# Two transformer layers on one core: modulation rows spread to one per weight slab, gates stored as sigmoids, gate halves loaded apart, attention steps moved a slab later

## The chip, the core and the metric

The kernel runs on one core of a Trainium2 chip, in fp32 from inputs to output. What counts is the device time of one execution, in microseconds (us). An engine's instructions run in its own order, and the engines wait for each other by semaphores: TensorE (PE) multiplies, VectorE (DVE) and ScalarE (ACT) do elementwise work, GpSimd (POOL) and SyncE (SP) issue most of the transfers from memory.

## The reference

256 tokens of width 2048 pass through two layers.

```python
# layer 1
mod = silu(c) @ w_ada + b_ada                 # 3 parts of 2048: shift, scale, gate
h = rmsnorm(x, pre_g) * (1 + scale) + shift
q, k, v, gate_a, u, gate_p = split(h @ w_in)
y_a = windowed_gqa(q, k, v) * silu(gate_a)    # 8 heads of 128
y_p = multiscale_pool(u) * silu(gate_p)
g_a, g_p = split(sigmoid(h @ w_merge + b_merge))
x = x + gate * rmsnorm((g_a * (y_a @ w_br_attn) + g_p * (y_p @ w_br_pool)) @ w_out)
# layer 2
mod = silu(c2) @ w_mod + b_mod                # 6 parts of 2048
...                                           # attention with 16 heads of 64, gated linear attention (GLA) with 4 heads
merged = sigmoid(g_a) * (o_a @ w_br_a) + sigmoid(g_b) * (o_b @ w_br_b)
x = x + g1 * rmsnorm(merged @ w_out)
h = rmsnorm(x) * (1 + sc2) + sh2
x = x + g2 * rmsnorm((silu(gate) * val) @ w_down)   # gate, val = conv(h @ w_up), width 5632
```

## The kernel before

**Weights in slabs.** All large products run as a row of 368 slabs, numbered through the program. A slab is 4 x 128 rows by 512 columns of weights, 1 MB. SP loads it to `w_stage` (5 buffers, `load_slab`, 3 slabs ahead). Since fp32 is multiplied as two halves of its bits, ACT rounds the slab to `w_hi` (`split_hi`, two instructions of 128x1024, 3 buffers), and DVE computes the rest to `w_lo` (`split_lo`, two instructions). Both do this `AHEAD` = 2 slabs before PE needs it, and `split_hi(n)` waits until PE has finished slab n-3. PE's `gemm(n)` runs 16 pairs of matmuls on a slab, (hi, 512 columns) and (lo, 256 columns), into the four PSUM tiles `gemm`. A group of 4 slabs (2 or 4 in the branches, 11 at the end) makes one result of 4 tiles. Then the group is evacuated in two pairs: ACT copies the low half out (`evac_low`), DVE adds the high half (`evac`), and the next group's first matmul on these tiles waits for that (`wait_evac`).

**Phases and hooks.** A `Phase` has one or two groups. All other work is tied to slabs of a phase: `hooks[s]` are run by every engine behind its part of slab s, `late` and `post` behind the phase, `pre` ahead of it. On each engine the order in a slab is: the split of slab s+2, the hooks of s, the modulation rows of s, and the evacuation if the group ends. Nothing else sets the order; each engine keeps to this list, and what waits holds up all behind it. The phases in order: u0, u1, in (4), in_gates (2), gate_p1, merge (8), branch1 (4), out1 (4), kv2, gk, q2 (2), qkvb (4), og (4), gates2 (4), branch2 (4), out2 (4), up (11), down (4). Ahead of u0, kv2 and up stands `prep_h`, which normalises and modulates h and makes its 16 operand tiles.

**Modulation rows.** `mod` is a vector times a matrix. Parts 0 and 1 are made before the first slab. Parts 2 to 8 are made beside the phases: a row is 128 x 2048 weights, loaded in two halves to `mod_stage` (one buffer for each half, `load_mod_row`: a half's load waits until DVE has used what stood there), and DVE adds it, times a column of c, to `mod_acc` (`mod_row`, two instructions of 128x1024). `mods_behind` spreads the rows of a phase evenly over the slabs that do not end a group; four rows on three such slabs put two behind the first. Behind a part's 16 rows PE sums over partitions (`mod_end`, 16 matmuls with one column each), and POOL clears `mod_acc`.

**Gates.** The merge gates of a layer are stored to memory before the sigmoid (`gate_out`, `store_gate`), as 8 groups of 4 tiles. In the phases branch1 and branch2 both halves (for the attention branch and for the other) are loaded together to `gate_in` when the phase before is merged, ACT takes the sigmoid of both (`gl_sig`), and `evac` multiplies with them, the first half behind slab 1.

**Attention.** A head (layer 1) or a pair of heads (layer 2) takes five steps: attn1 scores (PE); attn2 bias, row maximum (DVE) and exp (ACT); attn3 normalisation (DVE) and transposes (PE); attn4 copy (ACT) and product with v (PE); attn5 the operand (ACT, DVE). They stand behind slabs 0, 1, 2, 3 of a phase, and `late`. GLA has steps gla0 to gla7 in gates2; gla2 prepares on DVE and multiplies on PE behind the same slab.

Of the kernel before, what the change touches and what calls it, by code (L numbers as in the profile page):

```python
# [18 lines left out]
ALU = mybir.AluOpType  # L19
# [3 lines left out]
P = 128  # L23
# [70 lines left out]
class Phase:  # L94

    def __init__(self, name, i, groups, hooks=None, late=(), mod=None, pre=(), post=()):
        self.name, self.i, self.groups, self.hooks, self.late = name, i, groups, hooks or {}, late
        self.mod, self.pre, self.post = mod, pre, post
        self.slabs = [(g, q) for g in groups for q in range(g.slabs)]


def build(nc, A, out):
    ctx = ExitStack()
    with ctx:
# [119 lines left out]
        phases.append(Phase("gate_p1", 0, [one(4096)], mod=(3, 0, 3), post=[("silu1", 0), ("v1", 0)]))  # L224
        for i in range(8):
            arg = dict(blk=1, kv=i // 4, u=i)
            phases.append(Phase("merge", i, [Group(w_merge, 512 * i, 4, "main", "gate", bias=col["b_merge"] + 4 * i, slot=4 * i)],
                                hooks=attn(0, arg), late=[("attn5", arg)], mod=(3, 3 + 2 * i, 2) if i < 5 else (3, 8 + i, 1),
                                post=[("mod_end", 3)] if i == 7 else []))
        for i in range(4):  # L230
            phases.append(Phase("branch1", i, [Group(A["w_branch_attn"][0], 512 * i, 2, "attn", "merge_a", n=i),
                                               Group(A["w_branch_pool"][0], 512 * i, 2, "main", "merge_b", n=i)],
                                hooks={0: [("gl_sig", i)], **({2: [("merged_hi", (0, 0)), ("merged_hi", (0, 1))]} if i == 3 else {})},
                                mod=(4, i, 1), pre=[] if i else [("poolmix", 0), ("prep_y", 1)]))
# [1463 lines left out]
```

## Time and profile before

| | |
|---|---|
| median of 3 runs | 2533.04 us (2531.62 to 2541.36) |
| the profiled execution | 2532.78 us, span of its instructions 2531.0 us |
| mean granted clock of PE | 0.949 |
| busy: PE / DVE / ACT / POOL | 2313.1 / 1745.9 / 1103.2 / 93.8 us |
| moved | 580.55 MB, mean 229 GB/s |

Busy time is the time in which an instruction of the engine runs. The granted clock is the share of PE's full clock (2.4 GHz) that the chip lets through: 1.0, or 0.5 (1.2 GHz) after PE has stood still or done little; a mean over a stretch lies between. The profile gives times from the first instruction on. "Idle before, releaser" is the time an engine stood still before an instruction, and what ended it.

### The profile page before, as it was taken

What the parts mean: (1) busy time and instruction counts of PE and PEld (TensorE: products, weight loads), DVE (VectorE), ACT (ScalarE), POOL (GpSimd) and SP (SyncE); (2) the same over time, 40 slices, a digit from 0 to 9 for tenths busy, and PEclk for the clock granted to TensorE, in tenths of its full rate; (3) what the DMA queues carried; (4) which work ended last, traced back from release to release, by engine and by line L of the source; (5) the groups of instructions that cost most, each with busy time, mean ns of one, the idle gap of its engine ahead of it and who ended that gap; (6) DMA issues with size and microseconds to landing.
All of it is one profiled execution on the core that took longest, in us unless ns stands there. A gap on an engine that the chain in (4) does not pass through costs nothing. (4 is left out here: it accounts for less than half of the span.)

```text
span 2531.0 us, 31212 instructions
## 1 busy us (share of the span) xinstructions
PE 2313.1 (91%) x12880; PEld 1991.0 (79%) x12880; DVE 1745.9 (69%) x2015; ACT 1103.2 (44%) x1406; POOL 93.8 (4%) x112
## 2 busy tenths in 40 slices
PE   2499999999898899998999979988999999999998
PEld 1378788887777777787888868877888888888887
DVE  5877766767777677667766676776777777774443
ACT  1243344444445554443344443344444444444443
POOL 1000000010000000000011100000000000000000
PEclk7599999999999999998999989998999999999999
DMA  9967778776684756668866676784555555565553
GB/s 359 387 209 276 263 238 277 267 249 239 241 307 133 252 178 206 217 223 297 306 230 225 234 250 222 268 312 146 183 183 184 188 190 187 183 217 183 182 177 108
DMA packets 245089, 580.55 MB, mean 229 GB/s; under 512 B 11850, under 2 KB 14718, under 8 KB 240596
## 3 DMA queue, kind: packets, MB, share of 16 engines
q1 hardware_dynamic: 232320, 535.86, 61.3%
q0 software_dynamic: 11296, 40.20, 4.5%
q10 hardware_dynamic: 1332, 2.51, 0.3%
q8 instruction: 101, 1.65, 0.3%
q14 instruction: 40, 0.33, 0.0%
HBM read 557.55 MB, written 20.97 MB: 229 GB/s over the span
## 5 line engine op out<-in xcount | busy, mean ns | idle before, releaser
L1646 PE MATMUL gemm<-operand_main,w_hi 128*128 128x512 f32 x4311 | 1576.7, 406 | 82.1 <-DVE merge_part L1328 30.3
L1647 PE MATMUL gemm<-operand_main,w_lo 128*128 128x256 f32 x4311 | 1222.8, 284 | 0.0
L1015 DVE TENSOR_TENSOR w_lo<-w_stage,w_hi 128x1024 fp32r<-128x1024 f32 x736 | 860.9, 1212 | 468.9 <-ACT w_hi L670 468.2
L670 ACT ACTIVATE w_hi<-w_stage 128x1024 fp32r<-128x1024 f32 x736 | 732.6, 1045 | 783.7 <-PE gemm L1647 683.2
L1646 PEld LDWEIGHTS gemm<-operand_main,w_hi 128*128 128x128 f32 x4311 | 827.6, 192 | 279.6 <-DVE w_lo L1015 72.6
L1647 PEld LDWEIGHTS gemm<-operand_main,w_lo 128*128 128x128 f32 x4311 | 831.2, 193 | 13.6
L1009 DVE SCALAR_TENSOR_TENSOR mod_acc<-mod_stage,c_silu,mod_acc 128x1024 f32<-128x1024 f32 x224 | 280.9, 1281 | 83.1 <-DMA mod_stage<-in_w_mod 49.3
L1646 PE MATMUL gemm<-ffn_hidden,w_hi 128*128 128x512 f32 x688 | 242.9, 397 | 0.0
L1646 PE MATMUL gemm<-operand_attn,w_hi 128*128 128x512 f32 x480 | 181.2, 416 | 15.5 <-DVE proj L1316 15.5
L1647 PE MATMUL gemm<-ffn_hidden,w_lo 128*128 128x256 f32 x688 | 192.5, 280 | 0.0
L1646 PEld LDWEIGHTS gemm<-ffn_hidden,w_hi 128*128 128x128 f32 x688 | 129.1, 188 | 29.4
L1647 PE MATMUL gemm<-operand_attn,w_lo 128*128 128x256 f32 x480 | 139.0, 290 | 0.0
L1647 PEld LDWEIGHTS gemm<-ffn_hidden,w_lo 128*128 128x128 f32 x688 | 129.8, 189 | 0.8
L1646 PEld LDWEIGHTS gemm<-operand_attn,w_hi 128*128 128x128 f32 x480 | 95.5, 199 | 38.7 <-DVE w_lo L1015 16.7
L1650 PE MATMUL gemm<-operand_main,w_hi 128*128 128x512 f32 x313 | 125.5, 401 | 0.0
L1647 PEld LDWEIGHTS gemm<-operand_attn,w_lo 128*128 128x128 f32 x480 | 95.8, 200 | 1.6
L670 ACT ACTIVATE proj<-gemm 128x512 f32<-128x512 f32 (+1 forms) x73 | 43.3, 595 | 110.0 <-PE gemm L1650 109.9
L1649 PE MATMUL gemm<-operand_main,w_lo 128*128 128x256 f32 x313 | 88.7, 283 | 0.0
L1316 DVE TENSOR_TENSOR proj<-gemm,proj 128x512 f32<-128x512 f32 (+1 forms) x57 | 38.5, 685 | 54.0 <-ACT proj L670 54.0
L1649 PEld LDWEIGHTS gemm<-operand_main,w_lo 128*128 128x128 f32 x313 | 59.2, 189 | 15.4
L1322 DVE TENSOR_TENSOR gate_out<-gemm,gate_out 128x512 f32<-128x512 f32 x40 | 27.4, 691 | 54.4 <-ACT gate_out L670 54.3
L1650 PEld LDWEIGHTS gemm<-operand_main,w_hi 128*128 128x128 f32 x313 | 59.8, 191 | 0.0
(211 smaller groups left out, 1475.0 us busy)
## 6 DMA issues: line engine op xcount, KB each, us to landing
w_stage<-in_w_in SPq DMA_DIRECT2D x128, 1024.0 KB, 6.2
mod_stage<-in_w_mod SPq DMA_DIRECT2D x192, 512.0 KB, 6.0
w_stage<-in_w_up SPq DMA_DIRECT2D x88, 1024.0 KB, 5.0
w_stage<-in_w_down SPq DMA_DIRECT2D x44, 1024.0 KB, 5.0
w_stage<-in_w_ada SPq DMA_DIRECT2D x32, 1024.0 KB, 11.2
w_stage<-in_w_merge SPq DMA_DIRECT2D x32, 1024.0 KB, 6.0
w_stage<-in_w_out SPq DMA_DIRECT2D x32, 1024.0 KB, 7.8
mod_stage<-in_w_ada SPq DMA_DIRECT2D x32, 512.0 KB, 5.9
```

The source lines that it names most:

```text
L670: return nc.scalar.activation(o, i_, f, **kw)
L1009: stt(acc, MST[:, half, :], CSI[:, c:c + 1], acc, ALU.mult, ALU.add).then_inc(mod_rows, 1)
L1015: tt(WL[:, slot_of(n), c0:c1], WST[:, slot_of(n), c0:c1], WH[:, n % HIS, c0:c1].bitcast(F32), ALU.subtract)\
L1316: tt(o, high, o, ALU.add).then_inc(pair_done, 1)
L1322: tt(o, high, o, ALU.add).then_inc(pair_done, 1)
L1646: mm(G[:, m, :], hi, x_of(k), start=(k == 0), stop=False)
L1647: ins = mm(G[:, m, T:2 * T], lo, x_of(k)[:, 0:T], start=False, stop=False)
L1649: mm(G[:, m, T:2 * T], lo, x_of(k)[:, 0:T], start=False, stop=False)
L1650: ins = mm(G[:, m, :], hi, x_of(k), start=False, stop=True)
```

## The change

1. `slots` says behind which slabs the rows stand, at most one row per slab; the parts are dealt anew over the phases (og1 to og3 and out2 have 3 rows and no longer 4; gates2 has its rows late in a phase; mod_end of part 6 moves one phase on).
2. A part's first row is written by `tensor_scalar` and not added, so POOL's clearing of `mod_acc` is gone.
3. ACT takes the sigmoid of a gate group in `gate_out` before it is stored (`gate_sig`, behind slab 0 of the next phase, and behind slab 4 in gates2), 16 instructions of 128x1024. `store_gate` waits for it. `gl_sig` is gone.
4. The two halves of `gate_in` are loaded apart (`load_gates`), the attention half of phase i+1 as soon as that of phase i is multiplied.
5. PE's transposes (`attn_turn`) stand one slab later than DVE's attn3; attn4 and attn5 move behind slabs 0 and 1 of the next phase (slabs 4 and 5 within qkvb), the last head's stay `late`. The product with v goes to another PSUM tile, so that the next scores wait for less. PE's half of gla2 (`gla_pairs`) stands one slab later; gla7 moves from slab 1 to 2, the last head's gla6 and gla7 into branch2.
6. `poolmix`, `prep_y1` and `prep_y2` become hooks. 
7. In `prep_h` the splits of slabs 0 to 2 (0 to 3 in all) stand before or within the loop over operand tiles and not behind it.

```diff
-        attn = lambda o, a: {o + s: [(f"attn{s + 1}", a)] for s in range(4)}
+        attn = lambda o, a: {o: [("attn1", a)], o + 1: [("attn2", a)], o + 2: [("attn3", a)], o + 3: [("attn_turn", a)]}
+        def with_tail(hooks, at, a):
+            return {**hooks, at: [("attn4", a)] + hooks.get(at, []), at + 1: [("attn5", a)] + hooks.get(at + 1, [])}
...
-            phases.append(Phase("in_gates", i, [one(2048 + 1536 * i)], mod=((2, 11, 4), (2, 15, 1))[i],
+            phases.append(Phase("in_gates", i, [one(2048 + 1536 * i)], mod=((2, 11, 3), (2, 14, 2))[i],
...
-                                mod=(6, 4 * i - 4, 4) if i else (5, 14, 2), post=[] if i else [("mod_end", 5)]))
+                                hooks={} if i else with_tail({}, 0, head2[7]),
+                                mod=(6, 3 * i - 3, 3) if i else (5, 15, 1), post=[] if i else [("mod_end", 5)]))
...
-                                late=[("gla6", 3), ("gla7", 3)] if i == 3 else [], mod=((6, 12, 4), (7, 0, 3), (7, 3, 3), (7, 6, 3))[i], post=[] if i else [("mod_end", 6)]))
+                                       2: [("gla2", i)] + ([("gla7", i - 1)] if i else []), 3: [("gla_pairs", i)],
+                                       4: [("gate_sig", 8 + 2 * i), ("gla3", i)], 5: [("gla4", i)], 6: [("gla5", i)]},
+                                mod=((6, 9, 3), (6, 12, 4), (7, 0, 3), (7, 3, 3))[i], slots=(4, 5, 6, 2),
...
-            free = [n for n, (g, q) in enumerate(ph.slabs) if q < g.slabs - 1]
-            return [r for r in range(rows) if free[r * len(free) // rows] == s]
+            slots = ph.slots or [n for n, (g, q) in enumerate(ph.slabs) if q < g.slabs - 1]
+            return [r for r in range(rows) if sorted(slots[:rows])[r] == s]
...
+            def load_gates(blk, half, i):
+                n = i + 4 * blk
+                pool.wait_ge(gate_stored, 16 * ((0, 12)[blk] + 4 * half + i + 1))
+                if half:
+                    positive(pool, merge_tiles, 2 * n)
+                else:
+                    positive(pool, part_merged, n)
...
-                if name == "gl_sig":
-                    act.wait_ge(gates_in, 32 * arg + 32)
-                    activate(GL[:, :, :, :], GL[:, :, :, :], ACT.Sigmoid).then_inc(sig_ready, 1)
+                if name == "gate_sig":
+                    g = sig_groups[arg]
+                    o = GST[0 if arg < 8 else 1]
+                    wait_evac(act, g)
+                    activate(o[:, :, :], o[:, :, :], ACT.Sigmoid).then_inc(gate_sig, 1)
...
+                    for ahead in range(2 if k else 0, 3):
+                        split_lo(ph.slab0 + ahead)
...
+                        if s == 11:
+                            split_lo(ph.slab0 + 3)
```

DVE at the start of u0, before the change: the loop over operand tiles (`quad_work`, `operand_main`), then the splits (`w_lo`), 12 instructions on end. Rows are the instructions in the engine's order, with their lines.

```order
L1042 SCALAR_TENSOR_TENSOR affine_cols<-mod_cols,columns 128x16
L1058 SCALAR_TENSOR_TENSOR quad_work<-proj,affine_cols,rstd 128x256 x3
L1062 SCALAR_TENSOR_TENSOR operand_main<-quad_work,mod_cols,operand_main 128x256
...
L1062 SCALAR_TENSOR_TENSOR operand_main<-quad_work,mod_cols,operand_main 128x256 x3
L1015 TENSOR_TENSOR w_lo<-w_stage,w_hi 128x1024 x12
```

And with the change:

```order
L1086 SCALAR_TENSOR_TENSOR affine_cols<-mod_cols,columns 128x16
L1059 TENSOR_TENSOR w_lo<-w_stage,w_hi 128x1024 x6
L1106 SCALAR_TENSOR_TENSOR quad_work<-proj,affine_cols,rstd 128x256 x3
L1110 SCALAR_TENSOR_TENSOR operand_main<-quad_work,mod_cols,operand_main 128x256
...
L1059 TENSOR_TENSOR w_lo<-w_stage,w_hi 128x1024 x2
...
L1110 SCALAR_TENSOR_TENSOR operand_main<-quad_work,mod_cols,operand_main 128x256 x3
L1059 TENSOR_TENSOR w_lo<-w_stage,w_hi 128x1024 x4
```

Six halves (slabs 0 to 2) moved ahead of the loop, two (slab 3) into it.

DVE in the phase og2, before: the splits, the modulation rows (`mod_acc`, two instructions each) and the evacuation to `gate_out`.

```order
L1015 TENSOR_TENSOR w_lo<-w_stage,w_hi 128x1024 x2
L1009 SCALAR_TENSOR_TENSOR mod_acc<-mod_stage,c_silu,mod_acc 128x1024 x4
L1015 TENSOR_TENSOR w_lo<-w_stage,w_hi 128x1024 x2
L1009 SCALAR_TENSOR_TENSOR mod_acc<-mod_stage,c_silu,mod_acc 128x1024 x2
L1015 TENSOR_TENSOR w_lo<-w_stage,w_hi 128x1024 x2
L1009 SCALAR_TENSOR_TENSOR mod_acc<-mod_stage,c_silu,mod_acc 128x1024 x2
L1015 TENSOR_TENSOR w_lo<-w_stage,w_hi 128x1024 x2
L1322 TENSOR_TENSOR gate_out_87<-gemm,gate_out_87 128x512 x2
```

And with the change:

```order
L1059 TENSOR_TENSOR w_lo<-w_stage,w_hi 128x1024 x2
L1053 SCALAR_TENSOR_TENSOR mod_acc<-mod_stage,c_silu,mod_acc 128x1024 x2
L1059 TENSOR_TENSOR w_lo<-w_stage,w_hi 128x1024 x2
L1053 SCALAR_TENSOR_TENSOR mod_acc<-mod_stage,c_silu,mod_acc 128x1024 x2
L1059 TENSOR_TENSOR w_lo<-w_stage,w_hi 128x1024 x2
L1053 SCALAR_TENSOR_TENSOR mod_acc<-mod_stage,c_silu,mod_acc 128x1024 x2
L1059 TENSOR_TENSOR w_lo<-w_stage,w_hi 128x1024 x2
L1371 TENSOR_TENSOR gate_out_87<-gemm,gate_out_87 128x512 x2
```

The second row behind slab 0 is gone, the others stand where they stood.

ACT at slab 0 of gates2, phase 2, with the change: `gla_v` is gla6's sigmoid, the rows `gla_q` to `gla_k_end` gla0's exponentials. Before, the same rows stood there without the second one, and each ACT_TABLE_LOAD too.

```order
L701 ACTIVATE w_hi<-w_stage 128x1024 x2
L701 ACTIVATE gate_out_87<-gate_out_87 128x1024
L701 ACT_TABLE_LOAD
L701 ACTIVATE gla_rstd<-extra,small 128x256
L701 ACT_TABLE_LOAD
L701 ACTIVATE gla_v<-gla_out_gate 128x1024
L701 ACT_TABLE_LOAD
L701 ACTIVATE gla_q<-gla_diff 128x512
L701 ACTIVATE gla_k<-gla_diff 128x512
...
L701 ACTIVATE w_hi<-w_stage 128x1024 x2
```

One instruction, the sigmoid of the gate group before, moved in ahead of the table loads.

## Rows read from the trace of the kernel before

**Rows 1.** The page: busy time (parts 1 and 5).
```profile
PE 2313.1 (91%) x12880; PEld 1991.0 (79%) x12880; DVE 1745.9 (69%) x2015; ACT 1103.2 (44%) x1406; POOL 93.8 (4%) x112
L1009 DVE SCALAR_TENSOR_TENSOR mod_acc<-mod_stage,c_silu,mod_acc 128x1024 f32<-128x1024 f32 x224 | 280.9, 1281 | 83.1 <-DMA mod_stage<-in_w_mod 49.3
```

**Rows 2.** Windows at slab ends: us, busy (count), PEclk, DMA share, GB/s.
```profile
275.10:329.00 53.90, 47.75 (x259) 41.21 (x259) 33.48 (x30) 18.13 (x20) 0.00 (x0) 0.94 0.74 261
591.30:676.60 85.30, 74.04 (x386) 63.61 (x385) 57.76 (x63) 37.24 (x42) 4.49 (x6) 0.92 0.64 223
951.30:1115.40 164.10, 156.94 (x915) 129.82 (x915) 114.14 (x152) 77.43 (x138) 0.00 (x0) 1.00 0.61 212
1151.60:1234.10 82.50, 72.17 (x386) 62.34 (x385) 62.28 (x59) 29.57 (x34) 2.27 (x3) 0.94 0.93 328
1279.30:1291.70 12.40, 12.40 (x65) 11.30 (x66) 8.58 (x11) 9.89 (x12) 4.94 (x3) 0.72 0.41 139
1303.60:1311.00 7.40, 7.40 (x62) 6.59 (x62) 5.52 (x7) 2.61 (x3) 0.00 (x0) 1.00 0.47 154
1336.80:1452.40 115.60, 105.19 (x626) 91.87 (x625) 83.30 (x102) 54.84 (x64) 12.56 (x10) 0.96 0.66 227
1354.50:1368.70 14.20, 9.05 (x61) 8.00 (x62) 11.11 (x20) 2.61 (x3) 0.80 (x1) 0.88 0.39 137
1452.40:1579.20 126.80, 107.99 (x580) 93.08 (x578) 87.03 (x88) 55.44 (x60) 8.09 (x8) 0.91 0.68 233
1619.40:1733.50 114.10, 101.22 (x536) 86.77 (x534) 78.23 (x72) 47.60 (x59) 1.16 (x1) 0.94 0.80 281
1852.50:1897.80 45.30, 45.30 (x258) 39.29 (x257) 34.66 (x48) 20.41 (x22) 0.00 (x0) 1.00 0.57 186
```

**Rows 3.** Waits of PE: us in total, times, longest us.
```profile
PE gemm L1646 <- DVE merge_part L1328: 30.3, 7, 10.8
PE gemm L1646 <- DVE proj L1316: 28.3, 6, 6.6
PE gemm L1646 <- DVE w_lo L1015: 19.2, 4, 16.0
PE extra L1565 <- DVE scores L1237: 18.0, 11, 4.4
PE gemm L1646 <- DVE gate_out L1322: 10.3, 3, 3.7
PE extra L1601 <- DVE gla_k_end L1280: 7.6, 2, 3.8
```

**Rows 4.** Timeline of DVE at the start of u0.
```profile
115.97 1.28 DVE L1058 SCALAR_TENSOR_TENSOR quad_work<-proj,affine_cols,rstd 128x256 f32<-128x256 f32 x3
129.06 2.36 DVE L1015 TENSOR_TENSOR w_lo<-w_stage,w_hi 128x1024 fp32r<-128x1024 f32 x2 [0.34 <-ACT w_hi L670]
```

**Rows 5.** Timeline of DVE in og2.
```profile
1179.62 1.28 DVE L1009 SCALAR_TENSOR_TENSOR mod_acc<-mod_stage,c_silu,mod_acc 128x1024 f32<-128x1024 f32 x1 [2.72 <-DMA mod_stage<-in_w_mod]
```

**Rows 6.** DMA issues in 1145 to 1235: KB each, us to landing.
```profile
w_stage<-in_w_in SPq DMA_DIRECT2D x14, 1024.0 KB, 7.9
mod_stage<-in_w_mod SPq DMA_DIRECT2D x26, 512.0 KB, 5.3
```

**Rows 7.** Timeline of DVE in gates2, phase 3 (starts at 1394.6).
```profile
1407.11 2.36 DVE L1015 TENSOR_TENSOR w_lo<-w_stage,w_hi 128x1024 fp32r<-128x1024 f32 x2 [0.72 <-ACT w_hi L670]
1420.35 2.36 DVE L1015 TENSOR_TENSOR w_lo<-w_stage,w_hi 128x1024 fp32r<-128x1024 f32 x2
```

**Rows 8.** Timeline of ACT at its slab 0.
```profile
1397.09 1.28 ACT L670 ACT_TABLE_LOAD   x1
1398.39 0.48 ACT L670 ACTIVATE gla_rstd<-extra,small 128x256 f32<-128x256 f32 x1
```

**Rows 9.** Timeline of DVE in qkvb0.
```profile
921.69 0.69 DVE L1316 TENSOR_TENSOR proj<-gemm,proj 128x512 f32<-128x512 f32 x1 [0.97 <-ACT proj L670]
```

**Rows 10.** Lines of ACT by form: busy us, mean ns; idle before.
```profile
L670 ACT ACTIVATE gla_v<-gla_out_gate 128x1024 f32<-128x1024 f32 x4 | 4.2, 1061 | 0.0
```

More of the change, by code:

```diff
@@ L223, in build @@
                                 post=[("mod_end", 2)] if i else []))
-        phases.append(Phase("gate_p1", 0, [one(4096)], mod=(3, 0, 3), post=[("silu1", 0), ("v1", 0)]))
+        phases.append(Phase("gate_p1", 0, [one(4096)], mod=(3, 0, 2), slots=(1, 2), post=[("silu1", 0), ("v1", 0)]))
+        head1 = [dict(blk=1, kv=u // 4, u=u) for u in range(8)]
         for i in range(8):
-            arg = dict(blk=1, kv=i // 4, u=i)
+            behind = attn(0, head1[i])
+            if i:
+                behind = with_tail(behind, 0, head1[i - 1])
+                behind[0] = behind[0] + [("gate_sig", i - 1)]
+            if i == 6:
+                behind[2] = behind[2] + [("poolmix", 0)]
@@ L234, in build @@
-                                mod=(4, i, 1), pre=[] if i else [("poolmix", 0), ("prep_y", 1)]))
+                                hooks=behind, mod=(4, i, 1)))
         for i in range(4):
@@ L307, in build @@
                 merged_from.append(ph.slab0 + 2)
+        by_tile_phases = [ph for ph in phases if ph.name in ("u0", "kv2", "up") and ph.i == 0]
         named = lambda name: [ph for ph in phases if ph.name == name]
@@ L387, in build @@
         MA = proj_tile("merge_part", [P, QUAD, T], F32, 52)
-        gate_stored, gates_in, sig_ready = sem("gate_stored"), sem("gates_in"), sem("sig_ready")
+        gate_stored, gate_sig, part_merged = sem("gate_stored"), sem("gate_sig"), sem("part_merged")
+        gates_in = [sem("gates_a_in"), sem("gates_b_in")]
         merge_tiles = sem("merge_tiles")
+        sig_groups = [g for ph in phases if ph.name in ("merge", "gates2") for g in ph.groups]
         WP = proj_tile("w_pool", [P, 4, 2, 2 * P], F32, 40)
@@ L781, in stage @@
                     norm_root(n)
+                    if k == 0:
+                        for first_slab in range(3):
+                            split_hi(first_slab)
                     shift = (0, 3, 6)[k] * KT
@@ L957, in _ @@
                 for s, (g, q) in enumerate(ph.slabs):
-                    if ph.slab0 + s + AHEAD < len(slabs):
+                    if ph.slab0 + s + AHEAD < len(slabs) and not (ph in by_tile_phases and s < 2):
                         split_hi(ph.slab0 + s + AHEAD)
@@ L1627, in gemm @@
                     pe.wait_ge(op_ready, op_count[name] - g.slabs + q + 1)
-                if g.operand == "attn" and q == 0:
-                    pe.wait_ge(y_done, 8 if ph.name == "branch1" else 16)
+                if g.operand == "attn" and ph.i == 0:
+                    pe.wait_ge(y_done, 4 * q + 4 + (0 if ph.name == "branch1" else 8))
                 if g.operand == "hid":
```

151 lines of the change are left out of this document (86 added, 65 removed).

## The prediction

> **What bounds the kernel now.** I read the page first: PE is busy for 91% of the span, DVE for 69%, ACT for 44% [rows 1]. So PE is the bound, and the question is where it stands still. A window without a wait gives its pace: 8 slabs in 45.30 us at clock 1.00, 5.66 us a slab (5.65 below) [rows 2] (its last row). 368 slabs at that pace are 2079 us, so some 450 us are start, small matmuls, waits and half clock. The waits of PE name the waits [rows 3]: on the splits at the start (19.2, of which 16.0 once), on `merge_part` (30.3 in 7), `proj` (28.3 in 6), the attention's `scores` (18.0 in 11), `gate_out` (10.3 in 3) and GLA's `gla_k_end` (7.6 in 2).
>
> Then I cut the trace at slab ends. Last three phases of og: 82.50 us for 12 slabs, which are 67.8 at the pace [rows 2]. The loss is 14.7, the wait only 10.3 [rows 3]; the window's clock is 0.94. A wait of some 3.5 us thus costs about 1.5 more, because the granted clock then falls to its lower level (1.2 GHz) for a while: (14.7 − 10.3) / 3. Below, a wait of over 2 us counts with 1.5 to 1.7 more. The same subtraction prices each place.
>
> What is late there: DVE takes a half of a modulation row only when its transfer has landed (it waits 2.72 us for it) [rows 5], a half takes 5.3 us to land [rows 6], and there is one buffer for each half. All DVE has to do behind it, the evacuation last, waits too. What is removed is counted only where it frees this chain; DVE's 280.9 us on rows [rows 1] stay.
>
> **The change part by part.**
>
> *Start of u0.* The loop begins at 115.97 and the last splits at 129.06, which end at 131.4, when PE's wait ends [rows 4]. The six halves take 3 x 2.3 = 6.9 us and now stand ahead of the loop; ACT makes its halves while DVE and PE still work on `mod`, so I add nothing for it. The gemm may begin behind the first operand tile, about 1.6 us later: 115.97 + 6.9 + 1.6 = 124.5. Gain 131.4 − 124.5 = 6.9, say **7.0**. (The later operand tiles are made faster than PE takes a slab.)
>
> *Rows, at most one behind a slab.* Let a phase begin at T, the end of PE's slab before. ACT's and DVE's split put DVE's first row at about T + 3.4; the next row starts a landing plus 1.5 us later; so three rows, and the split behind them, end at T + 3.4 + 2 (L + 1.5) + 2.5 + 2.4 = T + 11.3 + 2L. With L = 5.3 [rows 6] that is T + 21.9, against four slabs' end T + 22.6; some semaphore steps add up to 1 us. It is about level, so I leave 1.0 a phase and no half clock. For og: 14.7 − 3 = 11.7, **12** with the few tenths that lie in front. in_gates: 53.90 − 8 x 5.65 = 8.7, leave 1: **7.5**. Out of layer 2: 114.10 − 16 x 5.65 − three `mod_end`-like sums of 1.7 = 18.6 [rows 2]; its first phase still has late rows behind a long evacuation, so I leave 6: **12.6**.
>
> *Gates.* In branch1 (12 slabs) 85.30 − 67.8 = 17.5 [rows 2], three waits on `merge_part` [rows 3]: ACT and DVE wait for both halves to land and ACT for its sigmoid. With the attention half loaded a phase early, and no sigmoid there, DVE has it ahead of time: **17.5**. Branch2 (18 slabs): 126.80 − 101.7 = 25.1 [rows 2], of which 10.8 idle is the first phase's [rows 3]. There ACT's chain stays long: two table loads of 1.28 and the new sigmoid of 1.06 [rows 8, 10] come before the operand and the split, and DVE follows 15.5 us behind the phase's start where PE needs it at 2 slabs, 11.3. 4.2 and 1.7 for the clock remain, about 6: **19.3**.
>
> The sigmoids cost 16 x 1.06 = 17 us of ACT [rows 10], which is idle 56% of the span [rows 1]; two table loads each more would be some 18 loads x 1.28 = 23 us. Both lie in slab 0, where ACT has more than 3 us to spare, but in gates2.
>
> *gates2.* The window of phases 2 and 3 is 115.60 us [rows 2]. A slab with GLA work and no wait is 7.40 [rows 2] (from 1303.60), slab 3 of phase 2 is 14.20, so 6.8 lost, twice: the two waits on `gla_k_end`, 3.8 each [rows 3], and 1.4 for `gla_k`. Moving PE's half a slab back removes both: +6.9 each. But the new sigmoid delays ACT's chain of three table loads by 1.06, and gla7 and a late row move to DVE's slab 2. For phase 3, from T = 1394.6: the splits that began at 1407.11 begin at T + 13.6; from there to the end of the splits of 1420.35 (1422.6) lie 15.5 us of DVE work [rows 7], of which one row of 2.4 moves away: T + 26.7, and 0.7 for the first evacuation. PE asks at 4 x 5.65 + 2.6 = T + 25.2. A new wait of about 2.2, with clock 3: net +3.9. Phase 1 has four rows, one in slab 2: wait 4.7 + 1.7 = −6.5, new. Phase 2 has `mod_end` (12.40 − 5.65 = 6.7, which leaves phase 1 [rows 2] (from 1279.30)) at its start, which gives DVE slack: +6.9. Sum **+4.3**. Without the cover of `mod_end` phase 2 would give 3 less.
>
> A rule of the Trainium skill speaks against this part. The row: a table load takes 1.28 us, from 1397.09, and the next ACT instruction starts at 1398.39, so 0.02 later [rows 8]. The page "ScalarE: Activation LUTs", section "What ACT_TABLE_LOAD costs", has 2.66 us for each switch, with a drain of 1.38. By the page the chain of loads would be some 4 us later at three places, and the result some 12 us higher, an estimate from that page. The trace disagrees with it here, and the sum goes by the row.
>
> *Attention.* The waits on `scores` are 18.0 in 11 [rows 3]: 5.1 in merge, 5.7 in qkvb0, and six of 1.2 later. Those of merge go with their clock, 5.1 + 1.6, less 1.1 of a new wait where the last head's product stands: **5.6**. qkvb1 to 3: 164.10 − 156.94 = 7.2 of idle at clock 1.00 [rows 2], all go. In qkvb0 DVE is late by itself: its evacuation starts at 921.69 [rows 9], where PE, freed of the wait, asks for it at 917.2; a wait of 4.1 takes its place. **6.9**.
>
> *prep_h of kv2 and up.* Splits in the loop remove the small waits behind its first slabs: **2.7**. A part's first row as `tensor_scalar` (half the time of a 1.28 us instruction at best, 14 of them) and POOL's clearing lie off the path: 0. poolmix and prep_y as hooks: 0, hidden behind slabs of PE; uncovered, some 2 us.
>
> Sum: 7.0 + 7.5 + 5.6 + 17.5 + 6.9 + 12 + 4.3 + 19.3 + 12.6 + 2.7 = 95.4. The profiled execution is 2532.78 us, 0.3 from the median of 2533.04. Time: 2532.8 − 95.4 = **2437 us**.
>
> Bounds of what the trace doesn't show: the left-overs of 1 us in rows (0 to 3.5 in 10 phases, −6 to +25), branch2's 6 (2 to 12), gates2's new waits (0 to 13 with clock, so −9 to +5), out's 6 (2 to 12). Together 2403 to 2470.
>
> **The rivals.**
> (A) *Clean:* all named gaps go and nothing takes their place: 12 + 6 + 9.5 + 4.1 + 3 of left-overs less, **2403**. For it: DVE has 31% free. Against it: the arithmetic in gates2 and branch20.
> (B) *The transfer stays the bound:* three rows in neighbouring slabs reload the same buffer, L is not 5.3 but 6 and more, and og, out2, in_gates and branch2 each keep 2 to 4 us a phase and the half clock. 7 to 10 phases of 3.5 more: **2465** (2455 to 2490). For it: slabs' loads land in 7.9 us in the same stretch [rows 6]. The page "Perfetto Trace Analysis" of the Trainium skill, section "Optimization Strategy", says that the same gap repeating can mean too few buffers. The change adds none.
> (C) *Slower:* the same mechanism, worse: with one row behind every slab L reaches what the slab loads take there, 7.9. Then three rows end at T + 27.1, 4.5 late, and with clock 6.2 in each of about 25 phases with three rows: 155 us, **2590**. It decides for slower from L = 7 (some 4.3 us a phase eats 108 us). Against it: L is 5.3 where the DMA share is already 0.93 [rows 2, 6], and halving the burst in slab 0 lowers it.
> (D) *It does nothing:* waits only change place, since DVE's work is the same: 2525 to 2540. Against it: branch1's wait is for a load that is simply earlier.
>
> **How the numbers follow.** Forecast 0.59 (2415 to 2455), A 0.15, B 0.19, C 0.04, D 0.03. All but C and D are faster by far over 0.5%, about what a measurement of this kernel can tell from none. The range takes the better part of A and half of B: 2400 to 2472. Faster 0.93, same 0.03, slower 0.04.
>
> **What would show it.** The first gemm's wait 9 in place of 16; no wait of over 1 us on `merge_part` in layer 1; in og and in_gates waits of at most 1 us; qkvb1 to 3 without idle time; a wait of 4.1 on `proj` in qkvb0; new waits on `gate_out` in gates2, phase 1 (4.7) and 3 (2.2); one of 4 on `merge_part` in branch20, and one of 4 at out21. mod_stage's landing at 5.3 to 6. I am wrong if this landing grows past 6.5, if DVE's splits come late where ACT loads tables, or if the clock falls in places where no wait is.

## The result, and the profile after

The changed kernel takes 2448.47 us in the median of 4 runs (2441.76 to 2450.23), the kernel before 2536.86 us beside it (2531.62 to 2541.36). The ratio is 0.9647, with a 95% interval of 0.9617 to 0.9678: faster, by 3.5% or some 88 us. I had forecast 2437 (2400 to 2472), 95 us less. The two profiled executions differ by 82.7 us of span (2531.0 and 2448.3); that of the changed kernel is the longest of its four (1.8 above their median), that of the kernel before lies 4.1 below its median, so the profiles show some 6 us less than the medians.

The page of the changed kernel, busy time by engine:

```profile
PE 2286.6 (93%) x12880; PEld 1973.2 (81%) x12880; DVE 1742.4 (71%) x2015; ACT 1125.4 (46%) x1432; POOL 81.2 (3%) x105
```

The waits of PE in the changed kernel, as [rows 3]:

```profile
PE gemm L1699 <- DVE proj L1365: 26.1, 7, 6.8
PE gemm L1699 <- DVE operand_main L1110: 17.8, 3, 9.5
PE gemm L1699 <- DVE gate_out L1371: 10.0, 4, 4.9
PE gemm L1699 <- DVE merge_part L1377: 5.3, 1, 5.3
PE gemm L1699 <- DVE proj L1377: 4.7, 3, 3.1
```

The waits on `scores` and `gla_k_end` are gone, that on `w_lo` of 16.0 is one of 9.5 on `operand_main`, and of seven on `merge_part` one is left; `proj L1377` is the evacuation of the other branch's half, at the ends of branch2's phases: three waits, 4.7 in all, that the kernel before didn't have. Those on `gate_out` are others than before: 4.9 and 2.5 of the 10.0 us are the new ones in gates2, and 2.1 is one behind merge's first phase that nothing had forecast:

```profile
371.45 0.47 PE L1699 MATMUL gemm<-operand_main,w_hi 128*128 128x512 f32 x1 [2.12 <-DVE gate_out L1371]
```

Windows of the changed kernel, cut at slab ends like [rows 2]. In order: in_gates, branch1, qkvb1 to 3, og1 to 3 with gates2's first slab, gates2 phase 1, gates2 phases 2 and 3, branch2's first three phases, out2; then two that gained nothing or little, q2's second phase and qkvb0.

```profile
268.80:314.50 45.70, 45.16 (x260) 39.22 (x258) 33.62 (x30) 18.25 (x20) 0.00 (x0) 1.00 0.83 288
575.30:643.00 67.70, 67.70 (x386) 58.85 (x385) 57.25 (x62) 32.51 (x39) 3.76 (x5) 1.00 0.81 279
919.10:1074.90 155.80, 154.20 (x914) 129.80 (x913) 114.84 (x153) 76.22 (x138) 0.00 (x0) 1.00 0.67 223
1111.80:1180.50 68.70, 68.08 (x386) 58.71 (x386) 53.05 (x51) 28.17 (x32) 2.27 (x3) 1.00 0.90 314
1225.60:1282.90 57.30, 52.40 (x316) 45.80 (x314) 44.66 (x53) 30.68 (x35) 6.28 (x5) 0.97 0.74 248
1282.90:1395.40 112.50, 109.99 (x656) 96.60 (x656) 83.85 (x103) 61.45 (x70) 13.60 (x11) 0.95 0.71 238
1395.40:1509.80 114.40, 105.32 (x579) 90.86 (x577) 92.73 (x91) 51.25 (x58) 7.70 (x8) 0.96 0.82 288
1548.80:1652.80 104.00, 98.20 (x536) 84.88 (x536) 77.71 (x74) 47.71 (x59) 1.16 (x1) 0.97 0.86 304
836.10:862.50 26.40, 24.35 (x129) 21.09 (x130) 20.81 (x20) 18.48 (x17) 0.00 (x0) 0.94 0.82 288
862.50:919.10 56.60, 52.16 (x291) 43.88 (x290) 41.50 (x56) 32.63 (x51) 0.00 (x0) 0.94 0.50 168
```

Read them against [rows 2]: the length less PE's busy time is idle time; what the length loses beyond that is half clock. Branch1 is 67.70 long, all busy, at clock 1.00: no wait is left. Out2 still has 5.8 idle and a clock of 0.97. Gates2 is counted over its phases 1 to 3, branch2 as forecast over its first three phases and then its last. Place by place, in us (forecast, then measured):

| place | forecast | measured |
|---|---|---|
| first product's wait | 7.0 | 6.5 |
| in_gates | 7.5 | 8.2 |
| merge, to the first product of branch1 | 5.6 | 2.1 |
| branch1 | 17.5 | 17.6 |
| qkvb | 6.9 | 10.7 |
| og to gates2's first slab | 12 | 13.8 |
| gates2 | 4.3 | 3.3 |
| branch2, first three phases | 19.3 | 12.4 |
| branch2, last phase | 0 | 1.2 |
| out2 | 12.6 | 10.1 |
| kv2, up | 2.7 | 2.6 |
| q2, second phase | 0 | −3.8 |
| the rest, by subtraction | 0 | −2.0 |
| sum | 95.4 | 82.7 |

### The profile page after: what moved, and what is told of

Its sections match the earlier page's. It is cut to its first block, busy times and chain, and to the rows that moved or that the text cites. A ratio compares the mean times of both kernels' runs of the same rounds, so it can differ in the third digit from the quotient of the medians.

```text
span 2448.3 us, 31291 instructions
## 1 busy us (share of the span) xinstructions
PE 2286.6 (93%) x12880; PEld 1973.2 (81%) x12880; DVE 1742.4 (71%) x2015; ACT 1125.4 (46%) x1432; POOL 81.2 (3%) x105
## 4 chain that ended last, share of the span: by engine, by line
PE 78%; DVE 11%; DMA 7%; ACT 2%; issue 1%; ACTq 0%; DVEq 0%; SPq 0%
PE gemm L1699 46%; PE gemm L1700 23%; DVE w_lo L1059 3%; PE gemm L1703 3%; DMA mod_stage<-in_w_mod 3%; DMA w_stage<-in_w_ada 3%; DVE mod_acc L1053 2%; PE gemm L1702 1%; PE extra L1499 1%; DMA w_stage<-in_w_in 1%; PE extra L1492 1%; ACT w_hi L701 1%; PE extra L1631 1%; DVE mod_acc L1038 1%; PE extra L1607 1%
## 5 line engine op out<-in xcount | busy, mean ns | idle before, releaser
L1699 PE MATMUL gemm<-operand_main,w_hi 128*128 128x512 f32 x4311 | 1560.6, 403 | 49.7 <-DVE operand_main L1110 17.8
L1700 PEld LDWEIGHTS gemm<-operand_main,w_lo 128*128 128x128 f32 x4311 | 824.4, 191 | 13.5
L1053 DVE SCALAR_TENSOR_TENSOR mod_acc<-mod_stage,c_silu,mod_acc 128x1024 f32<-128x1024 f32 x210 | 267.1, 1301 | 49.3 <-DMA mod_stage<-in_w_mod 43.1
L1699 PE MATMUL gemm<-operand_attn,w_hi 128*128 128x512 f32 x480 | 180.4, 415 | 15.3 <-DVE proj L1365 10.7
L1699 PEld LDWEIGHTS gemm<-operand_attn,w_hi 128*128 128x128 f32 x480 | 95.0, 198 | 38.6 <-DVE w_lo L1059 16.8
L1703 PE MATMUL gemm<-operand_main,w_hi 128*128 128x512 f32 x313 | 124.6, 398 | 0.0
L1700 PEld LDWEIGHTS gemm<-operand_attn,w_lo 128*128 128x128 f32 x480 | 95.4, 199 | 1.5
L1365 DVE TENSOR_TENSOR proj<-gemm,proj 128x512 f32<-128x512 f32 (+1 forms) x57 | 38.6, 684 | 48.4 <-ACT proj L701 48.4
```

The lines of the kernel that those rows point to most:

```text
L1053: stt(acc, MST[:, half, :], CSI[:, c:c + 1], acc, ALU.mult, ALU.add).then_inc(mod_rows, 1)
L1365: tt(o, high, o, ALU.add).then_inc(pair_done, 1)
L1699: mm(G[:, m, :], hi, x_of(k), start=(k == 0), stop=False)
L1700: ins = mm(G[:, m, T:2 * T], lo, x_of(k)[:, 0:T], start=False, stop=False)
L1703: ins = mm(G[:, m, :], hi, x_of(k), start=False, stop=True)
```

## The experiments

Each kernel was timed beside the kernel before; the numbers are medians, the ratio to the kernel before, and its 95% interval. Changes of single places are read from windows or waits, since those of the whole are only known to some 5 us.

**The rows dealt as before (e1_rows_old).**

```diff
-            slots = ph.slots or [n for n, (g, q) in enumerate(ph.slabs) if q < g.slabs - 1]
-            return [r for r in range(rows) if sorted(slots[:rows])[r] == s]
+            free = [n for n, (g, q) in enumerate(ph.slabs) if q < g.slabs - 1]
+            return [r for r in range(rows) if free[r * len(free) // rows] == s]
...
-                                mod=(6, 3 * i - 3, 3) if i else (5, 15, 1), post=[] if i else [("mod_end", 5)]))
+                                mod=(6, 4 * i - 4, 4) if i else (5, 14, 2), post=[] if i else [("mod_end", 5)]))
```

and so in every phase.

> The changed kernel with the rows dealt over phases and slabs as before (four rows in og1 to og3 and out2, the first two behind one slab; mod_end of part 6 behind gates2 phase 1's predecessor). Theory, that the rows' transfers set these phases: in_gates +7, og +14, out2 +10, branch2 up to +5 come back, while q2 gives 3.8 and gates2 phase 1 and 3 give their new waits (6.5 and 4) back: about +22, 2470 us. Rival, that the gates' and the attention's edits did most of it, since they take work from the same engines at the same places: under +8, 2456 us or less.

2480.20 us, ratio 0.9773 (0.9748 to 0.9797): 32 us slower than the changed kernel. Its windows of in_gates, og and out2:

```profile
269.10:324.60 55.50, 47.04 (x259) 40.73 (x259) 33.85 (x31) 18.25 (x20) 0.00 (x0) 0.94 0.71 252
1116.20:1198.50 82.30, 72.02 (x387) 61.85 (x386) 61.73 (x59) 29.47 (x34) 2.27 (x3) 0.94 0.92 326
1568.80:1684.30 115.50, 100.17 (x537) 85.86 (x535) 78.19 (x72) 47.72 (x60) 1.16 (x1) 0.94 0.79 278
```

They are as long as before the change ([rows 2]: 53.90, 82.50, 114.10), whatever else was changed. The deal of the rows alone is worth about 32 of the 88 us, more than the 22 I expected, since gates2 got 6 us slower and not faster. Two places got faster: q2's second phase went from 26.4 back to 22.6, and branch2's first three phases from 114.4 to 111.8.

**Is it the transfer or DVE's amount of work? (e5_old_two_buffers).** The kernel before, with a second pair of buffers for 12 rows.

```diff
+        MST2 = at("mod_stage_b", [P, 2, D // 2], F32, o_ex)
...
-                    sp.dma_start(MST[:, half, :], w.rearrange("(c q) n -> c q n", q=P)[row0 + r, :, c0:c0 + D // 2])\
-                        .then_inc(m_landed[half], 16)
+                    sp.dma_start(buf[:, half, :], w.rearrange("(c q) n -> c q n", q=P)[row0 + r, :, c0:c0 + D // 2])\
+                        .then_inc(landed_, 16)
```

> The kernel before, with its four rows in each of og1 to og3, but these 12 rows go alternately to mod_stage and to a second pair of buffers in memory that the attention left free. Theory, that the reload of a single buffer is what makes DVE late: the three waits on gate_out (3.6, 3.0, 3.7) and their half clock go, -13 to -15 in og and gates2's start, 2519 us. Rival, that four rows are too much work for DVE in four slabs: the waits stay at 3 and more, 2533 us.

2527.69 us, ratio 0.9956 (0.9938 to 0.9974), 11 us less: under the 13 to 15 expected, but clear of noise. The window of og and the landings in it (KB each, median us to landing):

```profile
1156.50:1224.60 68.10, 68.06 (x386) 58.87 (x386) 58.07 (x56) 27.86 (x31) 2.27 (x3) 1.00 0.97 363
```
```profile
mod_stage_b<-in_w_mod SPq DMA_DIRECT2D x10, 512.0 KB, 9.2
mod_stage<-in_w_mod SPq DMA_DIRECT2D x10, 512.0 KB, 6.6
```

With the four rows a phase of before, 82.50 became 68.10 without a wait. So DVE's amount of work was never too much (it is busy for 58.07 of the 68.10); the reload of a single buffer was what came late. A single landing takes longer here than the 5.3 of [rows 6], with more transfers under way at once, and it does not matter. Gates2's last two phases and out2 are 2 us longer each in this profile, which is the rest between 14 and 11; why isn't shown. The rival of the prediction that pointed to the buffers had the mechanism right; the deal cures it in another way, by asking for fewer rows.

**The load of the gates put off (e2_gates_late), the sigmoid put back (e7_sigmoid_in_branch), and both (e8_both_back).**

```diff
-                if half:
-                    positive(pool, merge_tiles, 2 * n)
-                else:
-                    positive(pool, part_merged, n)
+                positive(pool, merge_tiles, 2 * n)
```
```diff
+                if name == "gl_sig":
+                    half, n = arg
+                    act.wait_ge(gates_in[half], 16 * n + 16)
+                    activate(GL[:, half, :, :], GL[:, half, :, :], ACT.Sigmoid).then_inc(gl_ready[half], 1)
...
-                        dve.wait_ge(gates_in[int(b)], 16 * n + 16)
+                        dve.wait_ge(gl_ready[int(b)], n + 1)
```

> The changed kernel with one wait put back: the attention half of the gates is loaded no earlier than the other half, when the phase before is merged; the sigmoid stays ahead of the store. Theory, that the early load is what frees branch1: waits on merge_part of about 2 us come back (3.8 before, less the sigmoid of 1.9 that no longer follows the load) in three phases of branch1 and two of branch2, with some clock: +10 to +14, about 2460 us. Rival, that the sigmoid's leaving the chain was enough: the load of 4.7 us ends before slab 1's end, nothing comes back, 2449 us.

2445.22 us, ratio 0.9639 (0.9614 to 0.9665), 3 us less than the changed kernel. No wait came back in branch1: my theory was wrong, its rival right. In branch2 a wait went away, that of 3.1 at the second phase, though the rows stand as in the changed kernel; see branch2 in the next section.

> The changed kernel with the sigmoid taken on the loaded gates again, half by half, behind slabs 0 and 2 (3 in layer 2), while the early load stays; gates are stored as before the sigmoid. Theory of the sum: branch1 stays without waits, and in gates2 the chain of ACT is 1.06 shorter, so that the waits of 4.9 and 2.5 there become 3.9 and 1.5, and branch20's 5.3 becomes 4.2: -3 to -7, about 2444 us. Rival, that taking the sigmoid off the branches was needed: waits on merge_part of 1 to 2 us come back in branch1 and branch2, +5 or more, 2454 us.

2446.96 us, ratio 0.9634 (0.9617 to 0.9651), 1.5 us less than the changed kernel and less of a gain than expected. No wait in branch1 here either. The waits of PE that gates2 and branch20 have:

```profile
PE gemm L1704 <- DVE gate_out L1376: 8.4, 4, 4.0
PE gemm L1704 <- DVE merge_part L1382: 4.3, 1, 4.3
```

The longest wait on `gate_out` went from 4.9 to 4.0, that on `merge_part` from 5.3 to 4.3: the sigmoid's 1.06 us on ACT passes into PE's waits almost whole, as the prediction's arithmetic had it.

> The two edits of the runs before together: attention half loaded only when the phase before is merged, and its sigmoid taken in the branch phase, behind slab 0; the halves are still two loads and two sigmoids. Neither edit alone brought a wait back. Theory, that load, sigmoid and product are one chain and each edit alone is enough to shorten it: now waits on merge_part of 2 to 4 us return in three phases of branch1, and in branch2, +10 to +17, about 2460 us. Rival, that it was the joint load and the joint sigmoid of 1.9 behind slab 0, with the split of the next slab queued behind it: split in halves the chain stays short, no waits over 0.5 in branch1, 2447 us.

2455.68 us, ratio 0.9676 (0.9654 to 0.9697), some 7 us above the changed kernel and 9 to 10 above the runs with one of the two edits. Waits of PE:

```profile
PE gemm L1704 <- DVE merge_part L1382: 14.8, 6, 4.4
```

In branch1 three waits of 1.5 to 1.7 are back, of 3.6 to 3.8 before. Neither theory holds alone. The early load and the early sigmoid stand in for each other and together are worth 1.6 a phase; the other 2.1 are not in these two edits. What then still differs from the kernel before is that the halves are loaded and turned into sigmoids apart (1.06 us of ACT each, not 1.92 behind a joint load) and the deal of the rows. That it is the former I only argue: branch1 has one row a phase in both kernels.

**PE's transposes with DVE's step again (e3_turn_early).**

```diff
-        attn = lambda o, a: {o: [("attn1", a)], o + 1: [("attn2", a)], o + 2: [("attn3", a)], o + 3: [("attn_turn", a)]}
+        attn = lambda o, a: {o: [("attn1", a)], o + 1: [("attn2", a)], o + 2: [("attn3", a), ("attn_turn", a)], o + 3: []}
```

> The changed kernel with PE's transposes behind the same slab as DVE's attn3 again; the later attn4 and attn5 and the other PSUM tile stay. Theory, that PE waited there for DVE: the waits on scores come back, 1.2 in each of 16 steps of qkvb's and 0.6 or less in merge's: +8 to +10, about 2458 us, with one of 4 in qkvb0 in the place of today's on proj. Rival, that the waits went because the next scores wait for less: no wait on scores, 2449 us.

2456.22 us, ratio 0.9672 (0.9642 to 0.9702), about 7 above the changed kernel, somewhat under the theory's range of 8 to 10. Waits of PE:

```profile
PE extra L1618 <- DVE scores L1286: 13.5, 9, 4.6
```

The waits on `scores` come back (18.0 in 11 before, [rows 3]), 4.6 of them in qkvb0 where the changed kernel has its wait on `proj`. The six later ones are 0.5 to 0.7 each, not 1.2; so about half of those was the looser order of the later steps. Both reasons hold. The 13.5 us cost only some 7, since waits of DVE's evacuations on `proj` and `gate_out` shrink by 8.9 beside them.

**The splits behind the loop (e4_splits_behind).**

```diff
-                    for ahead in range(2 if k else 0, 3):
-                        split_lo(ph.slab0 + ahead)
...
-                        if s == 11:
-                            split_lo(ph.slab0 + 3)
```

> The changed kernel with the splits of the first slabs behind the loop over operand tiles again, in u0, kv2 and up. Theory, the sum's terms of 7.0 and 2.7: the first product's wait grows from 9.5 to 16 and small waits in slabs 2 to 4 of kv2 and up come back: +8 to +10, about 2458 us. Rival, that the start is bound by the operand tiles, and PE would wait for them in slab 0 instead: +3 or less.

2451.65 us, ratio 0.9663 (0.9627 to 0.9700): in the total hardly to be told from the changed kernel. Waits of PE:

```profile
PE gemm L1692 <- DVE w_lo L1054: 17.6, 3, 16.0
```

The wait of 16.0 is back in place of 9.5, so the term of 7.0 is 6.5; kv2 is 1.2 longer and up 0.5.

**What was left: rows moved (e6_rows_moved), rows lightened (e9_rows_lightened), the decay moved (e10_decay_moved).** The first takes q2's third row and phase 1's fourth row in gates2 away; the second also takes one row each from the first phases of branch2 and out2.

```diff
-                                mod=((6, 9, 3), (6, 12, 4), (7, 0, 3), (7, 3, 3))[i], slots=(4, 5, 6, 2),
+                                mod=((6, 9, 4), (6, 13, 3), (7, 0, 3), (7, 3, 3))[i], slots=(4, 5, 6, 2),
```
```diff
-                                mod=((7, 6, 3), (7, 9, 3), (7, 12, 4), (8, 0, 4))[i], slots=(4, 2, 3, 0) if i else (2, 3, 4),
+                                mod=((7, 6, 2), (7, 8, 4), (7, 12, 4), (8, 0, 5))[i], slots=(4, 2, 3, 0, 1) if i else (2, 3),
```
```diff
-                behind[1] = behind[1] + [("gk_ln", 0)]
-                behind[2] = behind[2] + [("gk_cum", 0)]
-                behind[4] = behind[4] + [("swap", 2)]
+                behind[0] = behind[0] + [("gk_ln", 0)]
+                behind[4] = behind[4] + [("swap", 2), ("gk_cum", 0)]
```

> The changed kernel with q2 at two rows a phase (as before) and four in gates2 phase 0 in place of phase 1. Theory, that a row too many makes these two waits: the wait at the start of q2's second phase (2.0 and 1.7 of clock) and the one of 4.9 in gates2 phase 1 shrink, the latter to about 2.4 or less; phase 0 has no gla7 before it and takes its row without a wait: -6 to -9, about 2441 us. Rival, that the fourth row only moves the wait: phase 0 shows 3 to 5 us instead, 2445 to 2449 us.

2442.32 us, ratio 0.9621 (0.9602 to 0.9639). This is 6 less than the changed kernel, as the theory had it. The wait at q2's second phase is gone and that of 4.9 in gates2 is 2.5. Gates2's phase 0 took its fourth row without a wait: from its second slab to its end it's busy throughout, as in the changed kernel. A wait of 0.9 in front of it belongs to og3's evacuation; in two kernels whose phase 0 has three rows (e8_both_back, e12_pool_clears) one of 1.1 and 1.0 stands there too.

```profile
PE gemm L1699 <- DVE gate_out L1371: 8.1, 4, 2.5
```

> The run with the moved rows (q2, gates2), and further: two rows in branch2's first phase (for three), four in its second, five in its last, two in out2's first. Theory, that the third row, behind a late start of DVE, makes the waits of 3.0 at branch2's second phase and of 4.9 at out2's: both fall under 1 us, -3.0 - 1.7 - 4.9 - 2.5 less 1 of new waits: -11 against the run with moved rows, about 2431 us. Rival, that these phases are late by the operands' preparation, whatever the rows: out2's wait stays over 3, -5 or less, 2437 us or more.

2436.79 us, ratio 0.9597 (0.9577 to 0.9616), 5.5 less than the run before it, not 11. Against the changed kernel, out2's second phase went from 32.1 to 25.3 and branch2's second from 38.6 to 33.9, as expected; the four rows in branch2's second phase then made a wait of 1.8 at the third, with half clock, 2.8 in all, and one of 1.1 at the fourth, 1.3. From branch2's first product to out2's it's 154.4 us, 1.5 less than in the run before; most of the gain is out2's.

> The changed kernel with the decay's logarithm (ACT) at slab 0 of the first qkvb phase instead of slab 1, and its two DVE instructions of 3.5 us at slab 4 instead of 2. Theory, that they put off the evacuation at slab 3: the wait on proj of 4.4 us there and its 3.4 at half clock go: -5 to -6, about 2443 us, with at most 1 us of wait left. Rival, that the wait moves to the evacuation at slab 7, since DVE gets the scans there too: -1 to +1, 2448 us.

2447.50 us, ratio 0.9642 (0.9621 to 0.9664). The window of qkvb0:

```profile
862.40:911.90 49.50, 49.50 (x290) 41.93 (x290) 40.29 (x54) 32.89 (x50) 0.00 (x0) 1.00 0.57 190
```

It lost 7.1 us and all its idle time, and the phase behind it gained 2.9 (its first wait grew from 1.6 to 3.0, with half clock). Half of each theory: the wait goes from slab 3, and part of it returns behind slab 7. In the median of the whole only 1.0 us is left, inside the noise; the profiled execution is the fastest of its four by 7.

**All of these together (e11_all),** with the sigmoid in the branch phases.

> All of what helped together: rows moved and lightened, decay moved, sigmoid in the branch phases with the early load. Theory, that the places are independent: -6 for the moved rows, -5 to -8 for the lightened, -5 for the decay, -2 to -3 for the shorter chain of ACT in gates2 and branch20: -20, about 2428 us. Rival, that the waits only wander: 2436 us or more.

2421.65 us, ratio 0.9540 (0.9520 to 0.9560): 27 us less than the changed kernel, 7 more than expected, 1.1% below it and the fastest here. Alone, the four parts had moved the medians by 6.2, 5.5, 1.0 and 1.5, which is 14; why the whole gives 27 isn't shown. Its profile, 25.5 shorter than the changed kernel's, has the difference in q2 (3.8), qkvb (5.9), og (1.0), gates2 (8.6), branch2's first three phases (3.1) and out2 (6.1), less 3.1 in in_gates, which no edit touches. Its page, and its window of out2 (all four phases, at full clock):

```profile
PE 2274.8 (94%) x12880; PEld 1964.5 (81%) x12880; DVE 1742.3 (72%) x2015; ACT 1101.5 (45%) x1414; POOL 81.0 (3%) x105
```
```profile
1527.60:1625.50 97.90, 95.66 (x537) 82.93 (x536) 76.59 (x72) 47.63 (x59) 1.16 (x1) 1.00 0.88 312
```

**POOL clears the sum again, the first row is added (e12_pool_clears).**

```diff
-                    if row0 + r == 0:
-                        ts(acc, MST[:, half, :], CSI[:, c:c + 1], None, ALU.mult).then_inc(mod_rows, 1)
-                    else:
-                        stt(acc, MST[:, half, :], CSI[:, c:c + 1], acc, ALU.mult, ALU.add).then_inc(mod_rows, 1)
+                    stt(acc, MST[:, half, :], CSI[:, c:c + 1], acc, ALU.mult, ALU.add).then_inc(mod_rows, 1)
```

> The changed kernel with POOL's clearing of mod_acc and the adding first row again. Theory of the sum: it lies off the path, DVE does 7 us more work in 14 instructions beside PE: 0, within 3 us of the changed kernel, 2446 to 2450 us. Rival, that the clearing held DVE at each part's start (some 2 us behind mod_end), and that part of what the rows gave is from it: +4 or more in the phases with a part's first row (merge0, branch1, q2, og1, gates2 phase 2, branch2's last), 2452 us or more.

2449.29 us, ratio 0.9645 (0.9625 to 0.9665), the same as the changed kernel within the noise. It was right to cost this edit at nothing.

## Why the prediction was right, and where it was off

**The bound and the method held.** PE is the bound before and after, and the excess lay in some thirty places. Pricing each as idle time plus what half clock adds gave 95 for 83 to 88. The total came out nearer than its parts: by the table the places forecast too high are off by 20 us and those forecast too low by 8, and that these offset each other was luck.

**Rows.** The step "Rows, at most one behind a slab" held in in_gates and og. Its cause, the single buffer, is shown by the run with two buffers, and its worth by the run with the old deal. Three places were missed: q2, branch2 and out2. As to q2, I went through the phases that lose rows and not through those that gain them. Its first phase has three rows where it had two. DVE in the changed kernel, third row of that phase:

```profile
831.28 1.29 DVE L1053 SCALAR_TENSOR_TENSOR mod_acc<-mod_stage,c_silu,mod_acc 128x1024 f32<-128x1024 f32 x1 [0.36 <-DMA mod_stage<-in_w_mod]
833.85 1.28 DVE L1053 SCALAR_TENSOR_TENSOR mod_acc<-mod_stage,c_silu,mod_acc 128x1024 f32<-128x1024 f32 x1 [1.29 <-DMA mod_stage<-in_w_mod]
835.05 2.35 DVE L1059 TENSOR_TENSOR w_lo<-w_stage,w_hi 128x1024 fp32r<-128x1024 f32 x2
```

The first row is on time (809.35), but the second began only at 826.16, behind the rotation of k, so that the evacuation came at 837.3 for a PE that asked at 836.1: a wait of 2.0 with the steps between, and 1.7 of clock. The formula T + 11.3 + 2L assumed a first row at T + 3.4 with the others one landing apart; where DVE comes late to the second, the third is late with it. Moving that row removed the wait.

**Branch2.** This is the largest miss, 19.3 for 12.4. The term left 6 in the first phase and nothing in the others. The first phase's wait is 5.3, not 4.2, and behind its three rows at slabs 2 to 4 stands one of 3.1 at the second phase, 4.7 with its clock. A row there waits 2.48 for its landing:

```profile
1424.79 1.28 DVE L1053 SCALAR_TENSOR_TENSOR mod_acc<-mod_stage,c_silu,mod_acc 128x1024 f32<-128x1024 f32 x1
1428.55 1.28 DVE L1053 SCALAR_TENSOR_TENSOR mod_acc<-mod_stage,c_silu,mod_acc 128x1024 f32<-128x1024 f32 x1 [2.48 <-DMA mod_stage<-in_w_mod]
```

Two things make this wait together, and the term had neither. One is the third row: the run with the lightened rows removed the wait. The other is edit 4 of the change, the early load of the gates' attention half, which now runs beside these rows. In the run with that load put off, the same row waits 1.03:

```profile
1422.94 1.28 DVE L1050 SCALAR_TENSOR_TENSOR mod_acc<-mod_stage,c_silu,mod_acc 128x1024 f32<-128x1024 f32 x1
1425.25 1.28 DVE L1050 SCALAR_TENSOR_TENSOR mod_acc<-mod_stage,c_silu,mod_acc 128x1024 f32<-128x1024 f32 x1 [1.03 <-DMA mod_stage<-in_w_mod]
```

The landings behind the first phase's wait in the changed kernel (1412 to 1440), then in that run (1410 to 1438):

```profile
mod_stage<-in_w_mod SPq DMA_DIRECT2D x4, 512.0 KB, 5.8
gate_in<-gates POOLq DMA_DIRECT2D x2, 512.0 KB, 6.6
```
```profile
mod_stage<-in_w_mod SPq DMA_DIRECT2D x4, 512.0 KB, 4.7
gate_in<-gates POOLq DMA_DIRECT2D x1, 512.0 KB, 5.9
```

And the second phase in both, from the end of the first (1436.4 and 1435.2):

```profile
1436.40:1475.00 38.60, 35.56 (x192) 30.66 (x192) 30.32 (x32) 14.32 (x16) 1.50 (x2) 0.96 0.85 295
```
```profile
1435.20:1469.20 34.00, 33.93 (x192) 29.49 (x193) 28.14 (x29) 13.98 (x16) 1.50 (x2) 1.00 0.91 315
```

The same holds in every kernel with three rows at these slabs: the wait is 2.6 to 3.3 where the half is loaded early and gone in the two where it isn't (gates late, both back), with landings of 5.5 to 5.8 against 4.6 and 4.7. From branch2's first product to out2's the run with the late load takes 150.0 us, the changed kernel 154.4. So putting off the early load, which branch1 doesn't need, gave branch2 4.4, and lightening its rows 1.5. The kernel with all edits still has the early load; what it would gain without it wasn't run.

That the 1.1 more in the first phase come from an instruction of POOL is argued in the last section, not shown.

**Gates.** Branch1's 17.5 came out as 17.6, but the reason given, the half that is loaded a phase early, is not the needed one: without it nothing was lost. The sigmoid moved ahead of the store was enough by itself, and so was the early load. A sum can be right with a step whose cause isn't the only one.

**gates2.** The new waits forecast at 4.7 and 2.2 are 4.9 and 2.5, and the run without the sigmoid there moved both by 0.95 (to 3.95 and 1.56). The chain of ACT at branch20's first slab in the changed kernel:

```profile
1397.79 1.05 ACT L701 ACTIVATE gate_out<-gate_out 128x1024 f32<-128x1024 f32 x1
1398.86 1.28 ACT L701 ACT_TABLE_LOAD   x1
1400.16 0.47 ACT L701 ACTIVATE gla_rstd<-extra,small 128x256 f32<-128x256 f32 x1
```

A table load still takes 1.28 and the next instruction starts 0.02 later, so the sum rightly went by [rows 8]. The 2.66 of the Trainium skill ("ScalarE: Activation LUTs", "What ACT_TABLE_LOAD costs") doesn't show on this path; by it, an estimate from that page, the wait in phase 3 would have been 2.5 + 3 x 1.38, some 6.6.

**qkvb** gave 10.7 for 6.9. In the last three phases 5.6 of the 7.2 of idle time went and not all: a wait of 1.6 on `proj` stands at the start of qkvb1, against the sign "without idle time". PE's busy time fell by 2.7 there (156.94 to 154.20), which the term left out; why it fell isn't shown. Qkvb0 gave 2.4, and by its own rows (5.7 of waits, 4.1 in their place) the term should have had 1.6 for it. Its wait of 4.1 on `proj` is 4.4. Moving the decay's two instructions shows its cause.

**Merge** gave 2.1 for 5.6. The waits on `scores` went (5.1), but two came: 2.1 on `gate_out` behind its first phase, which the term had at nothing, and the 1.0 forecast for the last head. With the rows dealt as before the first is 1.0, so about half of it comes from the new deal.

**Out2** gave 10.1 for 12.6: its second phase kept 4.9 idle, and 7 us with its clock, where I had left 6 for all. The third row of its first phase was the cause, as the lightened deal shows.

**The rivals.** The clean case (2403) failed at these places; no run here reached it. "The transfer stays the bound" was half true: its mechanism is shown, but q2, branch2 and out2 lost some 15 us by it (3.8, 4.7 and 6.8, part of which the sum had left in place) and not 28. The landing was 5.0 to 5.8 us beside q2, og and out2, and at most 6.7 beside a phase of branch2, above the limit of 6.5 that the prediction had named; but nowhere 7 in phase after phase, so the slower case was not near.

## What to carry to other kernels

When a stream of transfers shares one buffer with its consumer, reckon each phase as start + (items − 1) x (landing + use) + the last use, from the time at which the consumer really begins, and go through the phases that gain an item as well as those that lose one. A load that is started early runs beside others: look what it makes late there, and whether it's needed at all. A wait on the bound engine costs more than its length where the clock drops behind it, so many small waits are worth removing one by one; here the last 27 us came from moving a few rows, a sigmoid and the decay's instructions. Before a gain is put down to one of two edits, take back each alone and then both.

## What the runs showed of the hardware

**The clock after the same work is not always the same.** At the start of og1 stand the 16 one-column products of `mod_end`. The window of og1 is the same work in the changed kernel (first) and in the kernel with all edits (second), without idle time in either:

```profile
1099.50:1128.50 29.00, 29.00 (x160) 25.83 (x161) 16.93 (x17) 9.12 (x10) 0.77 (x1) 0.88 0.77 266
```
```profile
1091.40:1117.20 25.80, 25.80 (x160) 22.99 (x160) 16.93 (x17) 9.12 (x10) 0.77 (x1) 1.00 0.85 300
```

In one the granted clock fell towards its lower level behind them (mean 0.88), in the other it did not: 3.2 us. Over the same four slabs (1104.0 to 1128.6 in the changed kernel) it fell in six of the ten kernels whose og1 is the same (24.6 to 25.0 us) and not in the four others (22.6). Among the four is the run with the splits behind the loop, which has the changed kernel's work in og0 too. Similar steps of 1.3 to 2.9 show at gate_p1 and in gates2. Single profiles differ by some us for this reason alone.

**An instruction of DVE stands still while POOL multiplies.** In the changed kernel POOL's product of the output gate and DVE's second `gla_k_end`, which takes 0.35 alone:

```profile
1348.14 2.40 POOL L637 TENSOR_TENSOR gla_out_gate<-gla_out_gate,gla_v 128x1024 f32<-128x1024 f32 x1 [3.00 <-ACT gla_v L701]
```
```profile
1347.60 0.35 DVE L1310 TENSOR_TENSOR gla_k_end<-proj 128x192 f32<-128x192 f32 x1
1348.19 2.56 DVE L1310 TENSOR_TENSOR gla_k_end<-proj 128x192 f32<-128x192 f32 x1
```

It began 0.05 us behind POOL and ended 0.21 behind it. This repeats in each phase of gates2 that has a head before it, and in branch20, where two `operand_main` of 1.2 each take 3.79 beside POOL's 2.41; that is 1.4 us more than alone, ahead of the wait of 5.3. By the Trainium skill, "SBUF — State Buffer", section "Who interferes with whom", a DVE instruction with two inputs in SBUF contends with one of GpSimd that reads SBUF, for a shared port pair that is locked exclusively. The trace agrees: both instructions of DVE have two inputs in SBUF, and the one of 0.35 takes 2.56. No run here moved POOL's product away, so what it costs PE is not shown.
